# Gated delta groups: the forward substitution of the 16x16 blocks moved from VectorE to GpSimd, two weight splits placed later, the head-group loop written out

## The reference, cut to what matters

```
kb = k * beta[..., None]
vb = v * beta[..., None]
m = einsum('bhnid,bhnjd->bhnij', kb, k) * where(strict, decay, 0.0)
rhs = concatenate([vb, kb * exp(gc)[..., None]], axis=-1)
sol = triangular_solve(m + eye, rhs, left_side=True, lower=True, unit_diagonal=True)
u, w = sol[..., :dv], sol[..., dv:]
```

## Time and profile before

| | |
|---|---|
| median of three executions | 2154.03 us (2152.55 to 2160.12) |
| the profiled execution | 2150.23 us |
| its span in the profile | 2148.4 us |
| mean granted clock of TensorE | 0.951 of full speed |
| PE busy | 1951.1 us, 91% |
| PEld busy | 1620.1 us, 75% |
| DVE busy | 1018.5 us, 47% |
| ACT busy | 821.6 us, 38% |
| POOL busy | 684.8 us, 32% |

### The profile page before, as it was taken

One profiled execution on the slowest core, in us unless ns is written; L12 is line 12 of the kernel. 1 busy time (PEld: TensorE's weight loads), 2 busy tenths in 40 slices (PEclk: granted clock), 3 DMA queues, 4 the chain that ended last, 5 costly groups with the idle time before them and its releaser, 6 DMA issues.

```text
span 2148.4 us, 30354 instructions
## 1 busy us (share of the span) xinstructions
PE 1951.1 (91%) x11197; PEld 1620.1 (75%) x11269; DVE 1018.5 (47%) x1765; ACT 821.6 (38%) x1477; POOL 684.8 (32%) x334
## 2 busy tenths in 40 slices
PE   6999999799999979699699969988978999999994
PEld 4677777578778759688699969978967776777773
DVE  6422232613132255656746655575555455454544
ACT  4555632432232335226324523451335333333322
POOL 3132244343443422411431242125134212222212
PEclk9999999999999989889889989998989999999997
DMA  5112123132322303201301221131031111211111
GB/s 178 50 61 67 59 88 98 41 107 80 106 92 80 104 29 102 70 21 31 101 21 41 80 52 40 42 92 40 30 100 55 62 31 52 61 55 47 60 49 39
DMA packets 72898, 140.23 MB, mean 65 GB/s; under 512 B 30544, under 2 KB 40016, under 8 KB 72656
## 3 DMA queue, kind: packets, MB, share of 16 engines
q1 hardware_dynamic: 72064, 134.33, 20.2%
q10 hardware_dynamic: 720, 4.33, 0.5%
HBM read 129.13 MB, written 9.50 MB: 65 GB/s over the span
## 4 chain that ended last, share of the span: by engine, by line
PE 31%; issue 19%; POOL 8%; DVE 4%; ACT 2%; POOLq 0%; ACTq 0%; DVEq 0%
PE ps L301 6%; PE ps L302 6%; PE ps L303 6%; POOL wsp L296 5%; PE ps L2456 3%; PE ps L2425 2%; PE ps L2424 2%; POOL ov L644 1%; PE ps L2446 1%; PE ps L2161 1%; PE ps L2126 1%; POOL aux_f L655 1%; POOL work L655 1%; DVE aux_f L1358 1%; PE ps L2428 0%
## 5 line engine op out<-in xcount | busy, mean ns | idle before, releaser
L296 POOL TENSOR_TENSOR wsp<-raw,wsp 128x1024 fp32r<-128x1024 f32 x231 | 558.1, 2421 | 1282.1 <-ACT wsp L291 1282.1
L301 PE MATMUL ps<-h_split,wsp 128*128 128x264 f32 (+1 forms) x1488 | 524.5, 352 | 59.9 <-DVE ov L1409 41.0
L302 PE MATMUL ps<-h_split,wsp 128*128 128x264 f32 (+1 forms) x1488 | 511.5, 344 | 0.0
L303 PE MATMUL ps<-h_split,wsp 128*128 128x264 f32 (+1 forms) x1488 | 510.9, 343 | 0.0
L301 PEld LDWEIGHTS ps<-h_split,wsp 128*128 128x128 f32 x1488 | 289.3, 194 | 99.7 <-issue 56.2
L302 PEld LDWEIGHTS ps<-h_split,wsp 128*128 128x128 f32 x1488 | 288.9, 194 | 31.6
L303 PEld LDWEIGHTS ps<-h_split,wsp 128*128 128x128 f32 x1488 | 288.0, 194 | 32.4
L291 ACT ACTIVATE wsp<-raw 128x1024 fp32r<-128x1024 f32 x231 | 240.7, 1049 | 105.0 <-PE ps L303 103.7
L301 PE MATMUL ps<-y_split,wsp 128*128 128x512 f32 (+1 forms) x496 | 195.3, 394 | 12.9 <-DVE y_split L463 5.8
L302 PE MATMUL ps<-y_split,wsp 128*128 128x512 f32 (+1 forms) x496 | 191.7, 386 | 0.0
L303 PE MATMUL ps<-y_split,wsp 128*128 128x512 f32 (+1 forms) x496 | 191.0, 385 | 0.0
(11 more groups left out here) (346 smaller groups left out, 3237.1 us busy)
## 6 DMA issues: line engine op xcount, KB each, us to landing
raw<-in_w SPq DMA_DIRECT2D x231, 512.0 KB, 3.5
m_home<-ov SPq DMA_DIRECT2D x16, 256.0 KB, 4.4
x_home<-x_res ACTq DMA_DIRECT2D x1, 2112.0 KB, 6.7
x_res<-x_home ACTq DMA_DIRECT2D x4, 528.0 KB, 6.7
x_res<-in_x SPq DMA_DIRECT2D x4, 512.0 KB, 5.3
out<-x_res SPq DMA_DIRECT2D x8, 256.0 KB, 2.0
mats<-in_mats SPq DMA_DIRECT2D x1, 640.0 KB, 7.3
rope<-in_rope SPq DMA_DIRECT2D x1, 528.0 KB, 5.1
```

The lines of the kernel that those rows point to most:

```text
L296: pool.tensor_tensor(wsp[:, s, 1, :], raw[:, s, :], wsp[:, s, 0, :].bitcast(F32), ALU.subtract).then_inc(lo_ready, 1)
L301: pe.matmul(o, wh, xh, start=start, stop=False)
L302: pe.matmul(o, wh, xl, start=False, stop=False)
L303: return pe.matmul(o, wl, xh, start=False, stop=stop)
```

## The change

1. `substitute` leaves DVE. POOL does the same operations (`eliminate(k)`, L645 and L649 of the changed kernel; the diagonal is now a product of two constant blocks, L655; the transposition a product with ones, L663). `low(6)` stands between `eliminate(6)` and `eliminate(7)`, `low(7)` behind the transposition.
2. `low(8)` and `low(9)` go from ahead of `TN[c]` to ahead of the masks of joins 5 and 10.
3. PE's waits for `g_at` and `g_eabs` go from ahead of tile 9 to ahead of `level_0` at join 1.
4. `gdn_groups` takes the place of `mla_loop` for this layer: all four groups are written out on every engine, with constants where loop registers stood.

```diff
         def gdn_panel(j, g):
-            return (P_GDN + j, None, 0) if isinstance(g, int) and g == 0 else (P_GDN - 4 + j, g, 16)
+            return P_GDN + (16 * g - 4 if g else 0) + j, None, 0
+        def gdn_groups(group):
+            for g in range(NG):
+                group(g, g == 0)
...
-                for j in range(8):
+                w, wt = lane(lane_w), lane(lane_wt)
+                def eliminate(k):
+                    n = BLK - 1 - k
+                    tmp = lane_tmp[:, 0:n * k].rearrange("p (i j) -> p i j", j=k)
+                    below = w[:, k + 1:BLK, 0:k]
+                    pool.wait_ge(sem("g_lane"), gst(g, LANE_OPS, 2 * k - 1))
+                    pool.tensor_tensor(tmp, w[:, k + 1:BLK, k:k + 1].to_broadcast([P, n, k]),
+                                       w[:, k:k + 1, 0:k].to_broadcast([P, n, k]), ALU.mult)\
+                        .then_inc(sem("g_lane"), 1)
+                    pool.wait_ge(sem("g_lane"), gst(g, LANE_OPS, 2 * k))
+                    pool.tensor_tensor(below, below, tmp, ALU.subtract).then_inc(sem("g_lane"), 1)
+                for j in range(6):
                     low(j)
+                pool.wait_ge(sem("lanes_moved"), gst(g, ROWS_IN, LANES_IN))
+                if not first:
+                    pool.wait_ge(sem("z_lo"), gst(g, 4, 0))
+                pool.tensor_tensor(lane_w[:, 0:BLK * BLK:BLK + 1], mats[:, NEG_ONES, 0:BLK], mats[:, ONES, 0:BLK],
+                                   ALU.mult).then_inc(sem("g_lane"), 1)
+                for k in range(1, 7):
+                    eliminate(k)
+                low(6)
+                for k in range(7, BLK - 1):
+                    eliminate(k)
+                pool.wait_ge(sem("g_lane"), gst(g, LANE_OPS, LANE_OPS - 1))
+                pool.tensor_tensor(wt, w.rearrange("p i j -> p j i"),
+                                   mats[:, ONES, 0:1].unsqueeze(2).to_broadcast([P, BLK, BLK]),
+                                   ALU.mult).then_inc(sem("g_lane"), 1)
+                low(7)
...
-                low(8)
-                low(9)
...
+                    if s in (CHUNKS, 2 * CHUNKS):
+                        low(7 + s // CHUNKS)
...
-            mla_loop(pool, gdn_group)
+            gdn_groups(gdn_group)
...
-                substitute()
...
                 project(8, 0)
-                pe.wait_ge(sem("g_at"), gst(g, CHUNKS, 1))
-                pe.wait_ge(sem("g_eabs"), gst(g, CHUNKS * HG, CHUNKS * HG))
                 pe.wait_ge(sem("l2_ln"), gst(g, 4, 4))
                 project(9, 6)
...
                     if s == 1:
+                        pe.wait_ge(sem("g_at"), gst(g, CHUNKS, 1))
+                        pe.wait_ge(sem("g_eabs"), gst(g, CHUNKS * HG, CHUNKS * HG))
                         level_0()
```

More of the change, by code:

```diff
@@ L598, in gdn_group @@
                     weights(j)
-            for g in range(NG):
-                gdn_group(g, g == 0)
+            gdn_groups(gdn_group)
             rest = STREAM - RING - (P_KV - RING)
@@ L1026, in gdn_group @@
                     high_y(t)
-            mla_loop(act, gdn_group)
+            gdn_groups(gdn_group)
             def square_out(k):
@@ L1424, in level_0 @@
                        .then_inc(sem("g_t0"), 1)
[L1426 to L1444, removed]
                 def turned_16(c):
@@ L1632, in gdn_group @@
                 low_y(3)
-            mla_loop(dve, gdn_group)
+            gdn_groups(gdn_group)
             for m in range(8):
@@ L2289, in gdn_group @@
                 out_tile(7)
-            mla_loop(pe, gdn_group)
+            gdn_groups(gdn_group)
             pe.wait_ge(sem("g_vb"), CHUNKS * NG)
```

## The result

The changed kernel takes 2161.55 us (median of 20 runs, 2156.07 to 2170.20) against 2156.36 us for the kernel before (20 runs, 2151.50 to 2160.12): ratio 1.0026, 95% interval 1.0015 to 1.0038. It is 0.26% slower, 5.6 us by the ratio; the two medians differ by 5.2. The forecast was 2153.2 us with a range of 2138 to 2171 and "no change within 0.5%" as the likeliest case. The time lies in the range and in the band, but on the other side of zero from my sum of -0.8 us.

The account below looks back on a forecast made before the run. PE, busy 91% of the span, was taken as the bound, its waits ahead of join 0 deciding. Four groups losing 1.0 us each less the loop's 4.8 gave -0.8 us: 2153.2 us against the median, range 2138 to 2171.

Parts of the forecast that it names:

- steps 2 and 4: Substitution on POOL: diagonal and eliminations 1 to 6 take 4.3 us; eliminations 7 to 14 and transposition 6.3 us.
- The slower rival: Substitution on POOL: whole operations scale 1.85 times, 15.5 us in place of 10.6; 2173 us; chance 0.24 including beyond 2164.8.
- Step 7: SP's queue: 0.4 us to issue weights(9), then lane_w to row form in 6.25 us plus 1.2 for the panel.
- Step 8: POOL ahead of join 0: TN[c] and first mask take 7.6 us as before, join 0 starting 1.0 us later.
- the faster rival: Chain to join 0: DVE meetings, panel delay and operation gaps, together 4.3 us, do not come; 2136 us; chance 0.21 including under 2143.3.
- the 0.7 us of meetings with DVE: POOL's substitution: DVE's two gated operations exclude POOL at the shared port, 0.7 us taken between 0 and 1.4.
- Step 12: Loop written out: PE's issue gaps at the jumps go, 4.8 us won in all.
- Step 9: low(8) and low(9) at joins 5 and 10: POOL's idle time and masks made ahead cover them, costing nothing.
- Step 3: low(6) on POOL, 2.4 us: PE waits some 6 us ahead of tile 8, which costs nothing by itself.
- Step 11: PE's clock: it stands about as long in sum, one tile and first joins stay slow, no change.
- step 10: PE's moved waits and DVE's relief of 9.1 us: nothing beyond the other terms.
- Two weight splits hold up join 0, not the substitution: Before the change, POOL's low(8) and low(9), 5.17 us, lie on the chain ending last at join 0.

Follow-up runs that it names:

- r4: Changed kernel with low(7) moved from behind the substitution to straight behind low(6): ratio 0.9997 to the kernel before.
- r3: Changed kernel with SP's weights(9) moved from ahead of the lane_w writes to behind the row form's reads: ratio 0.9951 to the kernel before.
- r1: Kernel before with only the four groups written out on every engine: ratio 0.9974 to the kernel before.
- r5: Changed kernel with low(6) ahead of the substitution instead of inside it: ratio 0.9986 to the kernel before.
- r2: Kernel before, still in loop form, with only low(8) and low(9) moved to joins 5 and 10: ratio 0.9878 to the kernel before.
- r11: Kernel before with groups written out and low(8) and low(9) late, substitution still on DVE: ratio 0.9855 to the kernel before.
- r7: Kernel of r11 with PE's waits for g_at and g_eabs moved to join 1: ratio 0.9879 to the kernel before.
- r8: Changed kernel with low(8) and low(9) put back ahead of TN: ratio 1.0034 to the kernel before.

## Why the prediction was right or wrong

By its own steps, in group 1, times counted from the issue of the gather:

| step | forecast | measured |
|---|---|---|
| 1: landing of the gather | 3.0 | 3.0 |
| 2, 3, 4, 6: substitution with `low(6)` in it | 13.8 | 13.7 |
| 5: `low(7)` | 2.5 | 2.3 |
| 7: to `lane_w` out | 0.4 | 0.8 |
| 7: `lane_w` out to row form | 7.45 | 9.4 |
| 8: `TN[c]` and first mask | 7.6 | 8.0 |
| gather to join 0 | 34.7 | 37.2 |

- **The price of a small POOL operation** (steps 2 and 4) was right. The forecast was 0.25 us and 2.17 ns an element, 0.28 at 14 elements and 0.37 at 56; measured 0.29 and 0.37. The slower rival, by which the whole operation scales 1.85 times against DVE, gives 15.5 / 30 = 0.52 us an operation on average and is ruled out. By the rule of the Trainium skill, GPSIMD Engine Reference, section 4.1, GpSimd is about twice as slow for two inputs; the traces agree in direction, but for operations this small the ratio is 0.37 us to DVE's 0.25 a step, 1.5.
- **Step 7 failed.** I had named the panel ahead in the queue and set it at 1.2 us out of 0 to 3.3. From `lane_w` out to landing it took 8.5, 9.3, 8.4 and 8.5 us in the four groups, against 6.2, 6.2, 6.4 and 6.4 before: 2.0 to 2.3 us more in three groups, 3.1 in group 1, where two instruction transfers ran as well. r4 and r3 show it: the two writes took 1.7 and 1.8 to 1.9 us whenever no panel was just ahead of them, with the one exception told above. The 1.2 had no row behind it: it rested on the panel and the blocks sharing the DMA engines for a part only, which no run shows. What a trace shows is that the writes, with the panel just ahead, took 3.6 to 3.9 us each in the groups without an instruction transfer.
- Step 8 added 0.4 to 0.5 us in every group; SP's issue added 0.4 in group 1 and nothing in the others, where `lane_w` went out 0.42 us behind `low(7)`. `TN[c]` now meets `turned_16` on all four operations (6.75 us for four instead of 6.29), which step 8 left out of the sum, though the faster rival names it.
- Over the four groups join 0 lost 36.4 - 33.5 = 2.9 us each where I had 1.0. Four times 2.9 less the loop's 4.8 is +6.8 us, and the profiled spans differ by 6.1. The error of 1.9 us a group is the whole error of the forecast. About 1.2 of it is the panel of step 7 and 0.5 is step 8; the rest are small terms either way. The sum of -0.8 us was a small difference of two larger terms, so an error of this size in one of them turned its sign; that the time still fell inside the range is owed to the range's width.
- Of the signs, the time from the group's first `taps` to join 0 was 84.0 to 85.5 us against 83 forecast and 81.3 to 81.8 before. `lane_w` out less than 1 us behind `low(7)` was named as a sign of being wrong; it came in every group (0.42 and 0.81 us) and says little, since the 0.7 us of meetings with DVE had been added behind `low(7)` and fell inside the substitution. No sign was named for the way of `lane_w`, the step that failed.
- Step 12, the loop, was right: 4.8 forecast, 5.6 measured alone (r1).
- Step 9 was right: no wait for masks at joins 5 and 10, the joins are as long as before.
- Step 3 was right that PE's 6.6 us wait ahead of tile 8 costs nothing by itself. But the same `low(6)` on POOL's side cost 2.3 us a group, and it could have stood 4 us earlier for nothing (r5).
- Step 11 was right for the changed kernel, where the joins began at half clock before and after. It missed that this standing was itself a cost: in r2 and r11 the joins are 1.1 us a group shorter on average with join 0 at the full clock, and moving PE's waits (part of step 10, costed at nothing) loses 1.5 us a group on average once the row form is early enough (r7).
- "Two weight splits hold up join 0, not the substitution" was right (r2), and so was its consequence that the substitution then takes their place (r8).

## What to carry to other kernels

Before moving work to an idle engine, write down the chain of work that the next shared stage waits for and see on which engine it lies before and after. Here a chain that ran on DVE was moved onto POOL, which already carried the weight splits, and the last of these splits let a 512 KB panel go out just ahead of a 256 KB round trip. Ask of each part of a change whether it pays alone: one part here was worth 1.2%, another 0.3%, and a third hid them both. And a wait that looks removable may be what keeps TensorE busy just ahead of a stage of short dependent products. Read every group and not one: group 1, on which forecast and expectations rested, was the one with the longest way.

## What the runs showed of the hardware that was not expected

- A small load and a large one from one queue: 128 KB writes that land in 1.7 and 1.8 us by themselves took 3.6 to 3.7 and 3.8 to 3.9 us with a 512 KB load issued 0.4 us ahead (changed kernel, groups 0, 2 and 3), and the load 3.9 to 4.1.
- A 128 KB write took 3.7 us in r4, group 3, where one 16 KB instruction transfer of 1.6 us ran among its packets, and 1.8 in the other groups, where none did. In r3 the read of the row form took 4.8 and 5.2 us in the groups with such a transfer and 3.6 and 3.9 in those without. That these transfers delay the writes and reads is likely; no run was made to test it.
- A DVE operation with both inputs in SBUF was held until two GpSimd operations in a row had ended, 4.0 to 4.5 us for a 0.68 us mask, although other operations of the two engines advance side by side: in the changed kernel four `turned_16` on DVE took 5.68 us and four `TN[c]` on POOL 6.75 us in the same stretch. What decides which of the two happens was not tried.
- One measure of the clock's worth in this kernel: joins that begin 0.5 to 1.8 us behind a tile of 48 matmuls are 1.1 to 1.5 us shorter on average than the same joins behind 6 to 14 us of standing, 1.2 to 2.1 us in groups 0 to 2 and at most 0.3 in group 3.
